# The product of the S5 state with C two chunks later in TensorE's program

## The chip, the cores and the metric

The kernel runs on one core of a Trainium2 chip. The time is the device time of one execution in microseconds (us); less is better. The engines are TensorE (PE; its weight loads are listed as PEld), VectorE (DVE), ScalarE (ACT), GpSimd (POOL) and SyncE (SP), which issues the loads. Each runs its own program in order and waits for the others by semaphores.

## The reference

Two blocks follow each other on a sequence of 256 tokens of width 2048. The first is a hybrid layer with three branches (a spatial gating, an S5 state space branch, a cross attention over 256 memory rows), gates and an output product; the second a convolution module and a squared-ReLU MLP. The change touches the S5 branch alone:

```python
lam_bar = jnp.exp(lam * dt)
b_bar = ((lam_bar - 1) / lam)[:, :, None] * b_mat
bu = jnp.einsum('bsgh,gph->bsgp', uf.astype(jnp.complex64), b_bar)
_, states = lax.associative_scan(combine, (a_el, bu), axis=1)
y = jnp.einsum('bsgp,ghp->bsgh', states, c_mat).real + d.astype(f32) * uf
y = jax.nn.gelu(y.reshape(bsz, seq, BRANCH_W)).astype(u.dtype)
return y * jax.nn.sigmoid(y @ glu_w + glu_b)
```

There are 64 groups of 16 channels with 64 complex states each.

## The kernel before

Activations stand transposed, channels on partitions and the 256 tokens along the free dimension. All weights stream through the core once, in 680 **chunks** of 128 x 1024 numbers (512 KB). `plan()` writes their order out; chunk `c` is the unit of every engine's program, and each engine has a loop over `c`:

- SyncE loads chunk `c` into one of seven `raw` slots (`s_raw`) once chunk `c - 7` has been used.
- ScalarE writes the high part `wh` (L522, `s_hi`), into one of four slots, so the high part of chunk `c + 3` waits until TensorE has finished chunk `c - 1` (`s_mm`).
- VectorE subtracts and writes the low part `wl` (L875, `s_low_v`); it does so for chunk `c + 3` at the beginning of its step `c`. (In two other stages GpSimd does this.)
- TensorE waits for the low part of chunk `c` and multiplies: for most chunks eight pairs, `wh` by both parts of the activation (L1580) and `wl` by the high part (L1582).

Then, still in step `c`, ScalarE and VectorE evacuate the output tile that ended with chunk `c - 1` (L531, L906), apply gates (L537 and L911, L915; L587 and L948, L956, L959), and do the small work of the stage, in an order written out by hand: the softmax of the cross attention at steps 112 to 159, GELU from step 168 on (every 11 steps one tile), and S5.

The S5 branch runs at steps 81 to 240 (`S5 = 81`, `S5_STEP = 5`), beside the weight products of other branches. Its 32 groups of states take five steps each: group `n` is at step `i` when `c - 81 = 5 n + i`. Four groups make a tile `tt`. Its parts:

- `bu(tt)` on TensorE ahead of chunk 81 + 20 tt: the products of the input with B for four groups, into banks 3 to 6 (L1603).
- `s5_main` on VectorE: at i = 1 two multiplications read the group's bank (L1178, L1179; the second tells `s_m`); at i = 2 two sums and two scans (L1182 to L1188); at i = 3 two multiplications (L1193, L1194; the second tells `s_n`, after which GpSimd's `tables` may go on); at i = 4 the two state tiles are written (L1203, L1204, `s_n4`), after a wait for the previous tile's product with C (`s_cy`), which reads the same states. The first group of a tile uses bank 6.
- `cy(tt)` on TensorE: the product of the four groups' states with C, eight matmuls (16 rows of the trace) into bank 6 (L1614). It waits for the tile's last states (`s_n4`) and, by `s_m >= 4 tt + 5`, for the next tile's first group to have been read out of bank 6. It stands ahead of chunk 81 + 20 (tt + 1) + 2, that is 103, 123, 143, 163, 183, 203 and 223, and the eighth, for which no group follows, ahead of chunk 243.
- `s5_out(tt)` on VectorE: one instruction (L1208) adds the skip term and takes the product out of bank 6, in step i = 3 of the next tile's first group (L1190, L1191), the eighth time in step 244. It tells `s_s5y`, for which `bu(tt + 2)` and ScalarE's GELU of this tile wait, the last GELU in its step 245.

Of the kernel before, what the change touches and what calls it, by code (L numbers as in the profile page):

```python
# [136 lines left out]
def end(stage, t):  # L137
    return AT[stage, t].end
# [18 lines left out]
S5_SET, S5_SIN, S5_STEP = 50, 67, 5  # L157
BIAS = 36
S5 = 81
# [81 lines left out]
def _build(nc, a, out, ctx):  # L241
# [101 lines left out]
    def cv(name, i=0):  # L343
        off = C_OFF[name][0] + i
        return cst[:, off:off + 1]
# [7 lines left out]
    def states(tt, q):  # L353

        return wn[q] if q < 2 else (wn_early if tt < 4 else wn_late)[q - 2]
# [512 lines left out]
    def vector(e):  # L868
        w = Waits(e)

        def low(c):
            if c in ON_POOL:
                return
            w.wait_ge(s_hi, c + 1)
            e.tensor_tensor(wl[:, c % RAW, :], raw[:, c % RAW, :], wh[:, c % WN, :].bitcast(F32),  # L875
                            ALU.subtract).then_inc(s_low_v, 1)

        def tree():
            n = 16
            while n > 2:  # L880
                n //= 2
                e.tensor_tensor(sq0[:, 0:n, :], sq0[:, 0:n, :], sq0[:, n:2 * n, :], ALU.add).then_inc(s_v, w.own())  # L882
                w.wait_ge(s_v, w.n)
            e.tensor_tensor(sq0[:, 0:1, :], sq0[:, 0:1, :], sq0[:, 1:2, :], ALU.add).then_inc(s_sum, 1)

        def rstd(n, dst, eps):
            w.wait_ge(s_mean, n)
            e.tensor_scalar(dst, bank[7][:, 0:T], eps, None, ALU.add).then_inc(s_eps, 1)
            w.wait_ge(s_root, n)
            e.reciprocal(dst, dst).then_inc(s_rstd, 1)  # L890
# [275 lines left out]
        def s5_main(c):  # L1166
            n, i = divmod(c - S5, S5_STEP)
            tt, q = n // 4, Q_ORDER[n % 4]
            k, bv = 4 * tt + q, bank[S5_BANK[q]].rearrange("p (r t) -> p r t", r=2)
            cb = wcs[n % 2][:, 0:1, :].broadcast_to((128, 2, T))  # L1170
            sb = wcs[n % 2][:, 1:2, :].broadcast_to((128, 2, T))
            if i == 1:
                w.wait_ge(s_bu, tt + 1)
                w.wait_ge(s_tab, n + 1)
                w.wait_ge(s_s5, 1)
                if n >= 1:
                    w.wait_ge(s_n4, n)
                e.tensor_tensor(wm1, bv, cb, ALU.mult).then_inc(s_v, w.own())  # L1178
                e.tensor_tensor(wm2, bv, sb, ALU.mult).then_inc(s_m, 1)  # L1179
            elif i == 2:  # L1180
                w.wait_ge(s_m, n + 1)
                e.tensor_tensor(wm1[:, 0, :], wm1[:, 0, :], wm2[:, 1, :], ALU.add).then_inc(s_v, w.own())  # L1182
                e.tensor_tensor(wm1[:, 1, :], wm1[:, 1, :], wm2[:, 0, :], ALU.subtract).then_inc(s_v, w.own())
                rb = rr[:, k:k + 1].broadcast_to((128, T))
                w.wait_ge(s_v, w.n - 1)
                e.tensor_tensor_scan(wsc[:, 0, :], rb, wm1[:, 0, :], 0.0, ALU.mult, ALU.add).then_inc(s_v, w.own())
                w.wait_ge(s_v, w.n - 1)
                e.tensor_tensor_scan(wsc[:, 1, :], rb, wm1[:, 1, :], 0.0, ALU.mult, ALU.add).then_inc(s_v, w.own())  # L1188
            elif i == 3:
                if n >= 4 and n % 4 == 0:  # L1190
                    s5_out(tt - 1)  # L1191
                w.wait_ge(s_v, w.n)
                e.tensor_tensor(wm1, wsc, cb, ALU.mult).then_inc(s_v, w.own())  # L1193
                e.tensor_tensor(wm2, wsc, sb, ALU.mult).then_inc(s_n, 1)  # L1194
            elif i == 4:
                w.wait_ge(s_n, n + 1)
                w.wait_ge(s_cy, tt)
                if tt >= 4:
                    w.wait_ge(s_sc, 8)
                else:  # L1200
                    w.wait_ge(s_mm, end("v", 1))
                st = states(tt, q)
                e.tensor_tensor(st[:, 0, :], wm1[:, 0, :], wm2[:, 1, :], ALU.subtract).then_inc(s_v, w.own())  # L1203
                e.tensor_tensor(st[:, 1, :], wm1[:, 1, :], wm2[:, 0, :], ALU.add).then_inc(s_n4, 1)  # L1204

        def s5_out(t):
            w.wait_ge(s_cy, t + 1)
            e.scalar_tensor_tensor(uT[:, t, :], uT[:, t, :], cv("d", t), bank[6][:, 0:T], ALU.mult,  # L1208
                                   ALU.add).then_inc(s_s5y, 1)
# [239 lines left out]
        for c in range(1, NC + 1):  # L1449
            if c + 3 < NC and c != POST:  # L1450
                low(c + 3)
            if c == RX:
                rstd(1, r_x, 1e-6)
            if c in ENDED:
                evac(ENDED[c])
            if RX < c <= RX + 10:
                w.wait_ge(s_rstd, 1)
                scaled(c - RX - 1, Xf, "pre", r_x, s_xn, s_hh, hp, s_hl)
            if c == MEM_SQ + 4:
                w.wait_ge(s_mq, 4)  # L1460
                tree()
            if c == MEM_R:
                rstd(2, r_mem, 1e-6)
            if MEM_N <= c < MEM_N + 10:
                w.wait_ge(s_rstd, 2)
                scaled(c - MEM_N, Mf, "memg", r_mem, s_mn, s_mh, mp, s_ml)
            if S5_SET <= c <= S5_SIN:
                next(main_setup, None)
                if c == S5_SIN:
                    for _ in main_setup:  # L1470
                        pass
            if S5_SIN < c < S5:
                next(main_scales, None)
            if BIAS <= c <= BIAS + 4:
                bias_row(c)
            if LN_V <= c < Z:
                norm_v(c)
            if Z <= c < Z + 8:
                spatial(c)
            if ATT <= c < ATT + 48:  # L1480
                softmax(c)
            if S5 <= c < S5 + 32 * S5_STEP:
                s5_main(c)
            if c == S5 + 32 * S5_STEP + 3:
                s5_out(7)
            if GELU <= c < GELU + 8 * GELU_STEP:
                gelu(c)
            if c - 1 in ENDED and ENDED[c - 1].stage == "b1":
                t = ENDED[c - 1].t
                w.wait_ge(s_mgh, t + 1)  # L1490
                w.wait_ge(s_mg, 32 + t + 1)
                e.scalar_tensor_tensor(mgp.lo[:, t, :], Mf[:, t, :], 0.5, mgp.hi[:, t, :].bitcast(F32), ALU.mult,
                                       ALU.subtract).then_inc(s_mgl, 1)
            if c - 2 in ENDED and ENDED[c - 2].stage == "out" and c <= POST:
                out_second(ENDED[c - 2].t)
            if c - 1 in ENDED and ENDED[c - 1].stage == "out" and c <= POST:
                out_first(ENDED[c - 1].t)
            if OUT + 8 <= c < OUT + 24:
                t = c - OUT - 8
                w.wait_ge(s_xsq, t + 1)  # L1500
                if t == 0:
                    e.tensor_scalar(extra[1], scrB[7], 1.0, None, ALU.mult).then_inc(s_xsum, 1)
                else:
                    w.wait_ge(s_xsum, t)
                    e.tensor_tensor(extra[1], extra[1], scrB[7], ALU.add).then_inc(s_xsum, 1)
            if c == POST:
                out_first(15)
                out_second(15)
                post(c)
                e.tensor_scalar(cvs("wdw"), cvs("wdw"), 0.5, None, ALU.mult).then_inc(s_wdw, 1)  # L1510
            if c == POST + 1:
                w.wait_ge(s_w62h, 1)
                e.tensor_tensor(w62[1], cst[:, C_OFF["wdw"][0] + 14 * 31:C_OFF["wdw"][0] + 16 * 31],
                                w62[0].bitcast(F32), ALU.subtract).then_inc(s_w62l, 1)
            if P1 <= c <= P1_END:
                taps(c)
            if c in (PIVOT + 1, PIVOT + 2):
                centre(4 * (c - PIVOT - 1), 4)
            if c == LN2:
                norm_conv()  # L1520
            if c == FFN + 3:
                rstd(5, keep[1], 1e-5)
# [7 lines left out]
    def tensor(e):  # L1530
# [154 lines left out]
        for c in range(NC):  # L1685
# [14 lines left out]
            if Z <= c < Z + 8 and (c - Z) % 2 == 0:  # L1700
                i = (c - Z) // 2
# [12 lines left out]
            if S5 <= c < S5 + 32 * S5_STEP:  # L1714
                n, i = divmod(c - S5, S5_STEP)
                if i == 0 and n % 4 == 0:
                    bu(n // 4)
                if i == 2 and n % 4 == 0 and n >= 4:
                    cy(n // 4 - 1)
            if c == S5 + 32 * S5_STEP + 2:  # L1720
                cy(7)
            if c == POST:
                w.wait_ge(s_psum, 16)
# [110 lines left out]
```

## Time and profile before

| what | value |
|---|---|
| three runs | 2154.38, 2166.30, 2165.95 us, median 2165.95 us |
| the profiled execution | 2151.97 us, span 2150.2 us |
| TensorE, VectorE, ScalarE, GpSimd busy | 2025.2, 1653.2, 1015.5, 406.3 us |
| mean granted TensorE clock | 0.973 of full speed |
| S5 stage, first `bu` to last `cy` | 262 to 822 us of the span |
| there: TensorE, VectorE busy | 510.62 and 482.69 of 560 us, granted clock 0.96 |

Full speed of the clock is 2.4 GHz; 0.5 would be 1.2 GHz throughout. Times in the trace are from the start of the span. In a row of the timeline the bracket at the end is the idle time of that engine just before the instruction and what ended it.

### The profile page before, as it was taken

What the parts mean: (1) busy time and instruction counts of PE and PEld (TensorE: products, weight loads), DVE (VectorE), ACT (ScalarE), POOL (GpSimd) and SP (SyncE); (2) the same over time, 40 slices, a digit from 0 to 9 for tenths busy, and PEclk for the clock granted to TensorE, in tenths of its full rate; (3) what the DMA queues carried; (4) which work ended last, traced back from release to release, by engine and by line L of the source; (5) the groups of instructions that cost most, each with busy time, mean ns of one, the idle gap of its engine ahead of it and who ended that gap; (6) DMA issues with size and microseconds to landing.
All of it is one profiled execution on the core that took longest, in us unless ns stands there. A gap on an engine that the chain in (4) does not pass through costs nothing.

```text
span 2150.2 us, 30509 instructions
## 1 busy us (share of the span) xinstructions
PE 2025.2 (94%) x11898; PEld 1766.3 (82%) x11898; DVE 1653.2 (77%) x2630; ACT 1015.5 (47%) x1561; POOL 406.3 (19%) x281
## 2 busy tenths in 40 slices
PE   7899998999878989999889997999999999999997
PEld 6788887778767878888679996888888888888886
DVE  8766798988789986687889997777657656756765
ACT  5544443444433445556556634545434434434542
POOL 3400233433233330000158860000000000000000
PEclk9999999999989999999989998999999999999998
DMA  7554554444434545566435540555556555565563
GB/s 294 191 180 160 189 180 147 148 147 157 146 119 147 177 151 182 186 206 206 157 119 186 182 143 15 191 187 192 190 188 191 189 189 193 188 192 189 188 193 119
DMA packets 101519, 370.46 MB, mean 172 GB/s; under 512 B 11392, under 2 KB 11392, under 8 KB 101376
## 3 DMA queue, kind: packets, MB, share of 16 engines
q1 hardware_dynamic: 101376, 368.52, 52.6%
q8 instruction: 94, 1.54, 0.3%
q14 instruction: 49, 0.40, 0.1%
HBM read 366.38 MB, written 2.10 MB: 171 GB/s over the span
## 4 chain that ended last, share of the span: by engine, by line
PE 64%; DVE 27%; ACT 4%; issue 3%; DMA 1%; SPq 0%; DVEq 0%; ACTq 0%
PE bank L1580 38%; PE bank L1582 19%; DVE wl L875 7%; DVE bank L1382 6%; ACT wh L522 2%; PE bank L1570 1%; PE bank L1569 1%; PE bank L1571 1%; DVE scr L906 1%; DVE upad L988 1%; DVE sq L882 1%; DVE wm L1178 1%; PE bank L1614 1%; DVE wm L1179 1%; PE bank L1664 1%
## 5 line engine op out<-in xcount | busy, mean ns | idle before, releaser
L875 DVE TENSOR_TENSOR wl<-raw,wh 128x1024 fp32r<-128x1024 f32 x598 | 750.7, 1259 | 362.3 <-ACT wh L522 361.2
L522 ACT ACTIVATE wh<-raw 128x1024 fp32r<-128x1024 f32 x680 | 712.1, 1055 | 538.1 <-PE bank L1582 434.5
L1580 PE MATMUL bank<-Hr,wh 128*128 128x512 f32 x2432 | 869.8, 402 | 10.3 <-DVE wl L875 6.2
L1580 PE MATMUL bank<-Yr,wh 128*128 128x512 f32 x2240 | 792.3, 398 | 25.2 <-DVE wl L875 11.0
L1582 PE MATMUL bank<-Hr,wl 128*128 128x256 f32 x2432 | 683.5, 281 | 0.0
L1582 PE MATMUL bank<-Yr,wl 128*128 128x256 f32 x2240 | 626.8, 280 | 0.0
L1580 PEld LDWEIGHTS bank<-Hr,wh 128*128 128x128 f32 x2432 | 462.6, 190 | 129.0 <-issue 8.7
L1580 PEld LDWEIGHTS bank<-Yr,wh 128*128 128x128 f32 x2240 | 423.1, 189 | 129.6 <-DVE wl L875 11.4
L1582 PEld LDWEIGHTS bank<-Hr,wl 128*128 128x128 f32 x2432 | 464.1, 191 | 0.3
L1582 PEld LDWEIGHTS bank<-Yr,wl 128*128 128x128 f32 x2240 | 424.7, 190 | 0.2
L474 POOL TENSOR_TENSOR wl<-raw,wh 128x1024 fp32r<-128x1024 f32 x82 | 204.6, 2503 | 391.4 <-ACT wh L522 391.3
L1382 DVE SCALAR_TENSOR_TENSOR bank<-upad,cst,bank 128x256 f32<-128x256 f32 x406 | 164.9, 480 | 0.8
L1585 PE MATMUL bank<-Hr,wh 128*128 128x256 f32 x512 | 147.5, 288 | 12.2 <-DVE Hr L1361 11.5
L1586 PE MATMUL bank<-Hr,wh 128*128 128x256 f32 x512 | 146.2, 286 | 0.0
L1587 PE MATMUL bank<-Hr,wl 128*128 128x256 f32 x512 | 146.2, 285 | 0.0
L489 POOL TENSOR_TENSOR wcs<-tab 128x256 f32<-128x256 f32 x32 | 40.6, 1268 | 486.4 <-DVE wm L1194 344.3
L1585 PEld LDWEIGHTS bank<-Hr,wh 128*128 128x128 f32 x512 | 99.5, 194 | 14.1 <-issue 7.8
L1586 PEld LDWEIGHTS bank<-Hr,wh 128*128 128x128 f32 x512 | 99.7, 195 | 0.0
L1587 PEld LDWEIGHTS bank<-Hr,wl 128*128 128x128 f32 x512 | 99.7, 195 | 0.0
L665 ACT ACTIVATE Yr<-scrB 128x256 fp32r<-128x256 f32 x64 | 26.8, 418 | 146.6 <-DVE scrB L1018 146.6
L587 ACT ACTIVATE scr<-scr 128x256 f32<-128x256 f32 x32 | 13.4, 418 | 97.8 <-DVE scr L906 97.8
L1021 DVE TENSOR_TENSOR Yr<-scrB,Yr 128x256 fp32r<-128x256 f32 x64 | 27.2, 425 | 31.0 <-ACT Yr L665 31.0
(287 smaller groups left out, 1756.5 us busy)
## 6 DMA issues: line engine op xcount, KB each, us to landing
raw<-in_w_up SPq DMA_DIRECT2D x128, 512.0 KB, 4.3
raw<-in_w_dn SPq DMA_DIRECT2D x128, 512.0 KB, 4.3
raw<-in_w_g SPq DMA_DIRECT2D x96, 512.0 KB, 3.7
raw<-in_w_p SPq DMA_DIRECT2D x96, 512.0 KB, 3.7
raw<-in_w_b SPq DMA_DIRECT2D x48, 512.0 KB, 3.7
raw<-in_w_out SPq DMA_DIRECT2D x32, 512.0 KB, 4.3
raw<-in_w_bx SPq DMA_DIRECT2D x16, 512.0 KB, 4.9
raw<-in_w_q SPq DMA_DIRECT2D x16, 512.0 KB, 3.9
```

Of the source, the lines that this page charges most:

```text
L474: e.tensor_tensor(wl[:, c % RAW, :], raw[:, c % RAW, :], wh[:, c % WN, :].bitcast(F32), ALU.subtract).then_inc(s_low_g, 1)
L489: e.tensor_tensor(d[:, 0, :, :], *sides(0, 0), ALU.mult)
L522: e.activation(wh[:, c % WN, :], raw[:, c % RAW, :], ACT.Copy).then_inc(s_hi, 1)
L665: e.activation(hid.hi[:, t % 16, :], kept(j), ACT.Copy).then_inc(s_hidh, 1)
L875: e.tensor_tensor(wl[:, c % RAW, :], raw[:, c % RAW, :], wh[:, c % WN, :].bitcast(F32), ALU.subtract).then_inc(s_low_v, 1)
L1021: e.tensor_tensor(hid.lo[:, t % 16, :], s, hid.hi[:, t % 16, :].bitcast(F32), ALU.subtract).then_inc(s_hidl, 1)
L1382: e.scalar_tensor_tensor(ac, pad[:, j:j + T], wj, ac, ALU.mult, ALU.add).then_inc(s_v, w.own())
L1580: e.matmul(dst.rearrange("p (h t) -> p h t", h=2), lh, pair.both[:, :, k, :], start=first_part and kk == 0, stop=last_part and kk == 7, sk ...
L1582: ins = e.matmul(dst[:, 0:T], ll, pair.hi[:, k, :], start=False, stop=last_part and kk == 7, skip_group_check=True)
L1585: e.matmul(dst[:, 0:T], lh, pair.hi[:, k, :], start=first_part and kk == 0, stop=False)
L1586: e.matmul(dst[:, 0:T], lh, pair.lo[:, k, :], start=False, stop=False)
L1587: ins = e.matmul(dst[:, 0:T], ll, pair.hi[:, k, :], start=False, stop=last_part and kk == 7)
```

## The change

`cy` moves from step i = 2 to step i = 4 of the next tile's first group in TensorE's program, so behind two more chunks (ahead of chunks 105, 125, 145, 165, 185, 205 and 225); the eighth moves from chunk 243 to 244. `s5_out` moves from i = 3 of that group to i = 1 of the one after it, three steps later, the eighth time from step 244 to 245. The waits inside the functions stay.

```diff
@@ s5_main (VectorE)
             if i == 1:
+                if n >= 5 and n % 4 == 1:
+                    s5_out(tt - 1)
                 w.wait_ge(s_bu, tt + 1)
@@
             elif i == 3:
-                if n >= 4 and n % 4 == 0:
-                    s5_out(tt - 1)
                 w.wait_ge(s_v, w.n)
@@ vector
-            if c == S5 + 32 * S5_STEP + 3:
+            if c == S5 + 32 * S5_STEP + 4:
                 s5_out(7)
@@ tensor
                 if i == 0 and n % 4 == 0:
                     bu(n // 4)
-                if i == 2 and n % 4 == 0 and n >= 4:
+                if i == 4 and n % 4 == 0 and n >= 4:
                     cy(n // 4 - 1)
-            if c == S5 + 32 * S5_STEP + 2:
+            if c == S5 + 32 * S5_STEP + 3:
                 cy(7)
```

## Rows read from the trace of the kernel before

**Rows 1.** The page's sums: busy us (share of the span), instructions.

```profile
PE 2025.2 (94%) x11898; PEld 1766.3 (82%) x11898; DVE 1653.2 (77%) x2630; ACT 1015.5 (47%) x1561; POOL 406.3 (19%) x281
```

**Rows 2.** TensorE's waits, 260 to 870: total us, times, longest us.

```profile
PE bank L1614 <- DVE wm L1179: 33.9, 6, 7.3
PE bank L1580 <- DVE wl L875: 5.3, 6, 1.6
```

**Rows 3.** Windows, the six idle stretches: length, busy us of each engine, clock, DMA.

```profile
core 0: us, PE busy (x) PEld busy (x) DVE busy (x) ACT busy (x) POOL busy (x), PEclk, DMA share, GB/s
328.64:335.77 7.13, 0.00 (x1) 0.03 (x1) 6.96 (x10) 3.21 (x5) 2.37 (x4) 0.78 0.22 75
469.18:471.67 2.49, 0.01 (x1) 0.04 (x2) 2.27 (x6) 1.36 (x3) 0.00 (x0) 1.00 0.59 194
...
755.67:761.60 5.93, 0.00 (x0) 0.03 (x1) 5.86 (x8) 2.35 (x4) 3.42 (x4) 0.81 0.27 92
sum 33.90, PE 0.01 PEld 0.19 DVE 29.39 ACT 14.93 POOL 10.45; mean PE 0.00 PEld 0.03 DVE 4.90 ACT 2.49 POOL 1.74
```

**Rows 4.** Windows, product and next chunk at these six sites.

```profile
471.67:477.10 5.43, 5.43 (x33) 4.25 (x34) 3.50 (x7) 0.15 (x1) 0.00 (x0) 0.69 0.04 16
...
761.60:767.58 5.98, 5.98 (x33) 4.20 (x33) 3.17 (x6) 0.72 (x2) 0.00 (x0) 0.62 0.00 0
sum 36.05, PE 36.04 PEld 25.89 DVE 20.49 ACT 2.02 POOL 0.00; mean PE 6.01 PEld 4.32 DVE 3.42 ACT 0.34 POOL 0.00
```

**Rows 5.** Windows, product and next chunk at the eighth site.

```profile
821.38:825.32 3.94, 3.94 (x34) 2.98 (x34) 2.51 (x3) 1.37 (x2) 0.00 (x0) 1.00 0.44 140
```

**Rows 6.** Timeline of VectorE, 328 to 343: start, us, instruction.

```profile
331.29 2.35 DVE L875 TENSOR_TENSOR wl<-raw,wh 128x1024 fp32r<-128x1024 f32 x2
...
334.94 0.68 DVE L1179 TENSOR_TENSOR wm<-bank,wcs 128x512 f32<-128x512 f32 x1
335.54 1.22 DVE L875 TENSOR_TENSOR wl<-raw,wh 128x1024 fp32r<-128x1024 f32 x1
```

**Rows 7.** Timeline of VectorE, its idle time behind the six stalls.

```profile
342.72 1.23 DVE L875 TENSOR_TENSOR wl<-raw,wh 128x1024 fp32r<-128x1024 f32 x1 [4.11 <-ACT wh L522]
...
478.45 1.22 DVE L875 TENSOR_TENSOR wl<-raw,wh 128x1024 fp32r<-128x1024 f32 x1 [3.06 <-ACT wh L522]
...
553.55 1.22 DVE L875 TENSOR_TENSOR wl<-raw,wh 128x1024 fp32r<-128x1024 f32 x1 [4.77 <-ACT wh L522]
...
631.55 1.22 DVE L875 TENSOR_TENSOR wl<-raw,wh 128x1024 fp32r<-128x1024 f32 x1 [4.51 <-ACT wh L522]
...
700.47 1.23 DVE L875 TENSOR_TENSOR wl<-raw,wh 128x1024 fp32r<-128x1024 f32 x1 [2.74 <-ACT wh L522]
...
768.93 1.23 DVE L875 TENSOR_TENSOR wl<-raw,wh 128x1024 fp32r<-128x1024 f32 x1 [4.16 <-ACT wh L522]
```

**Rows 8.** Timeline of ScalarE, 341 to 342.

```profile
341.63 1.06 ACT L522 ACTIVATE wh<-raw 128x1024 fp32r<-128x1024 f32 x1 [9.78 <-PE bank L1582]
```

**Rows 9.** Timeline of TensorE, its waits for VectorE between the stalls.

```profile
378.76 0.44 PE L1635 MATMUL bank<-ident,Pb 128*128 128x128 f32 x2 [2.45 <-DVE Pb L1288]
...
578.24 0.51 PE L1580 MATMUL bank<-Hr,wh 128*128 128x512 f32 x1 [0.45 <-DVE wl L875]
...
669.45 0.50 PE L1580 MATMUL bank<-Hr,wh 128*128 128x512 f32 x1 [0.26 <-DVE wl L875]
...
742.83 0.50 PE L1580 MATMUL bank<-Hr,wh 128*128 128x512 f32 x1 [1.15 <-DVE wl L875]
```

**Rows 10.** Timelines of VectorE and TensorE: chunk 242's low part and first matmul.

```profile
814.81 1.22 DVE L875 TENSOR_TENSOR wl<-raw,wh 128x1024 fp32r<-128x1024 f32 x1
...
818.46 0.40 PE L1580 MATMUL bank<-Hr,wh 128*128 128x512 f32 x1
```

**Rows 11.** Line L1208: duration min/median/max ns, first and last start.

```profile
L1208 DVE SCALAR_TENSOR_TENSOR uT<-uT,cst,bank x8: 472/475/477, 346.1 to 828.1; 128x256 f32<-128x256 f32 x8
```

**Rows 12.** Windows, 570 to 610.

```profile
570.00:610.00 40.00, 33.15 (x177) 27.43 (x177) 34.92 (x56) 18.49 (x33) 11.45 (x12) 0.96 0.45 145
```

## The prediction

> **What bounds the kernel now.** I read the page's sums first. TensorE is busy for 94% of the span and VectorE for 77% [rows 1]: the kernel is TensorE's, but a share over 2150 us says nothing about one stage, so the next view is who TensorE waits for in the S5 stage. There one line stands out: 33.9 us in front of the product with C (L1614), in six of its eight calls, and each time the releaser is L1179, VectorE's second multiplication out of bank 6 [rows 2]. In the code this is the wait of `cy` for `s_m`: the product writes bank 6 and may not start before step i = 1 of the next group has read it. `cy` stands ahead of chunk 5n+2 of the stage where n is a multiple of 4, and that reading belongs to VectorE's step just one chunk earlier, so VectorE has less than one chunk for it. The waits for the low parts of the weights (L875) come to only 5.3 us [rows 2].
>
> The stretches themselves say more. Six idle stretches sum to 33.90 us, and VectorE is busy for 29.39 us of them [rows 3]: it is not idling, it is behind. The clock pays too. From the start of the product to the end of the chunk behind it the six stalled sites take 36.05 us, at granted clocks like 0.62 and 0.69 [rows 4]; the last site, which did not wait, takes 3.94 us at 1.00 [rows 5]. So 36.05 - 6 x 3.94 = 12.4 us goes to matmuls at 1.2 instead of 2.4 GHz after the idling. At most 33.9 + 12.4 = 46.3 us is to be had.
>
> What can be had depends on VectorE. After a stall it runs out of work: it waits 4.11, 3.06, 4.77, 4.51, 2.74 and 4.16 us for the first high part that ScalarE could not write while TensorE stood still, in sum 23.4 us [rows 7]; ScalarE had waited 9.78 us for TensorE at the first of them [rows 8]. Between the stalls VectorE loses that lead again, until TensorE waits for it: for a softmax weight behind the first site (2.45 us), for low parts behind the third, fourth and fifth (0.45, 0.26, 1.15 us) [rows 9]. Where such a tie comes before the next site, the gain is what VectorE gained, not what TensorE gained.
>
> **The change, part by part.** *The product moves two chunks later.* There are eight: the six that stall, and two that don't. It asks for the same `s_m` with two chunks more to cover it. One chunk at full clock takes 3.94 us less about 1.0 us for the product, so 2.9 us [rows 5]. The first site worked out: TensorE ends chunk 102 at 328.64, takes chunk 103 at once until 331.5, waits about 1 us for chunk 104's low part (the first of the pair that ends at 333.64), ends chunk 104 at 335.4 and finds L1179 done at 335.62 [rows 3, 6]. So 7.13 us of idle time go, about 1.2 us of new waits come, and with the site's share of the clock, 12.4 / 6 = 2.1 us, TensorE wins about 8 us. VectorE, though, wins 4.11 us [rows 7], and the tie at 378.76 [rows 9] hands on only that.
>
> The six sites, in order:
> - site at 335.77: 4.1 us (VectorE's idle time, tie at 378.76);
> - site at 471.67: 2.49 us idle [rows 3] + 5.43 - 3.94 = 1.5 us of clock [rows 4, 5] = 4.0 us. VectorE is not behind here (it idles 3.06 us after the stall, and more later), so TensorE keeps all of it;
> - site at 545.94: 4.8 us (tie at 578.24);
> - site at 623.55: 4.5 us (tie at 669.45);
> - site at 692.99: 2.7 us (tie at 742.83);
> - site at 761.60: 5.93 us idle + 5.98 - 3.94 = 2.0 us of clock, less about 0.3 us of new wait, is 7.6 us; VectorE gains 4.16 us and had a lead of 818.46 - 816.03 = 2.4 us at the thinnest place, chunk 242, whose low part is the fifteenth after the one at 768.93 [rows 7, 10]. So 4.2 + 2.4 = 6.6 us.
>
> Sum: 4.1 + 4.0 + 4.8 + 4.5 + 2.7 + 6.6 = 26.7, say **27 us**. Lower bound: VectorE's idle time alone, 23.4 us. Upper bound: 46.3 us less the new waits at the new place, about 1 us at four sites, so 42 us. I take 27, near the lower end, since three ties in a row show VectorE as the limit between 570 and 745.
>
> *What asks for the product.* VectorE's step i = 4 waits for `s_cy` before it overwrites the states that the product reads. Before, this product was two chunks old; now TensorE issues it in the very step. Queued behind that wait are the next low part and so TensorE. The cover: this step begins with a low part whose high part needs the chunk ahead of the product, and these two take 1.06 + 1.22 us [rows 7, 8] against about 1.0 us for the product. No cost; without the cover at most 1 us x 8. The step works later than that wherever VectorE is behind.
>
> *The evacuation (L1208, 475 ns [rows 11]) moves from step 3 to step 1 of the next group.* The same eight instructions, 3.8 us, on the same engine. They leave the way of L1193/L1194, which release GpSimd's tables, and enter that of L1178/L1179 of a group whose readers are no longer close. Between -0.5 and +0.5 us at each of eight sites; I take 0. The next product with B (`bu`) waits for `s_s5y` 14 chunks later. The eighth evacuation now falls in the VectorE step in which ScalarE's last GELU asks for it, one step earlier before: ScalarE may wait one low part and the evacuation, 1.22 + 0.48 = 1.7 us, with the next high part queued behind. TensorE gets no stall from this while low parts are 2 us ahead: 0, at most 1.7 us. No DMA is moved; the weight loads hang on `s_mm`, and follow the chunks.
>
> **Against the times.** The profiled execution takes 2151.97 us, 1.8 us over its span; with the sum it would take 2125 us. The shown median, 2165.95 us, lies 14 us above it. I carry the difference over: 2166 - 27 = **2139 us**, a gain of 1.25%.
>
> **Rivals.**
> *All of it is kept (TensorE is the limit).* If VectorE finds slack where TensorE runs into it, 42 us: 2124 us. For it: 5.3 us only of waits for low parts over the stage. Against it: these waits are few because the six stalls refill VectorE's lead. 12%.
> *The wait comes back.* VectorE is busy for 34.92 of 40 us between 570 and 610 [rows 12], and part of its remaining idle time comes from round trips through ScalarE which no earlier TensorE shortens. If half of the 23.4 us goes the same way, 12 us stay: 2154 us, within 1%. Against it: the idle times of rows 7 end on a high part that waited for TensorE alone. 18%.
> *Slower, by the clock.* The six long waits become many short ones in front of low parts. If TensorE then ran at 1.2 GHz through the tied stretches, it would fall behind VectorE. A product with its chunk at a granted 0.62 takes 5.98 against 3.94 us [rows 4, 5], 2.0 us more; 13 such chunks undo the 27 us, and 24 of the 120 between the first and the last stalled product make it 1% slower, 2188 us. Against it: from 570 to 610 TensorE already waits in this way, busy for 33.15 of 40 us, and the granted clock is 0.96 [rows 12]. 5%.
> The Trainium skill ("TensorE: Matmul & The Clock Gate", section "A second HAM failure mode: psum-queue depth-cycling") tells of a kernel whose TensorE idled briefly between groups of matmuls so often that the clock swung between its two levels and throughput fell. By that rule the tied stretches would swing too, and the sum would end near the 2188 us of this rival; the trace shows it only in small, with 0.96.
> *It does nothing.* Were the true releaser another semaphore, asked for as late at the new place, the time stays: 2166 us, 3%. Against it: `s_n4`, the other wait of `cy`, is told by a step two before that of L1179, and the profile names L1179 six times in six [rows 2].
>
> **How the numbers follow.** Forecast 62%. A measurement of this kernel tells about 1% (22 us) from no change. Of the forecast's own range, 20 to 34 us, a little lies below that; with the full gain this makes faster 0.68, within 1% 0.27, slower 0.05. The range runs from 2112 us (the full gain of 42 us on a run like the lowest one shown, 2154) to 2154 us (half of it given back); beyond it lie the slower case, no effect, and the poorer half of the third.
>
> **What the changed profile should show.** The 33.9 us in front of L1614 fall under 5 us, and the granted clock behind the products is mostly 1.00. VectorE's six idle times of rows 7 are gone or under 2 us. TensorE's other waits for VectorE grow by 10 to 19 us (46.3 us that were lost less 27 us won), above all for L875, in the stretches behind the stalled products. The S5 stage, from the first `bu` to the last `cy`, gets shorter by 27 us, and nothing else changes. Wrong would be: a wait of VectorE at L1203 for the product; a granted clock under 0.9 over whole stretches; or L875 waits of 30 us, which would mean that VectorE's own work, not the place of one wait, sets the stage.

## The result, and the profile after

The changed kernel takes 2124.41 us (median of 4, 2123.11 to 2138.78) beside 2160.16 us for the kernel before (median of 4); the ratio is 0.9875, with a 95% interval from 0.9838 to 0.9912. (The quotient of the two medians alone would be 0.983; 7 to 27 later executions of the kernel before have medians of 2151.47 to 2151.99 us, and beside those the change wins 27 us.) Its profiled execution takes 2123.11 us, its span 2121.4 us against 2150.2 us: 28.8 us less, where the sum had said 27. Single runs of either kernel now and then take some 13 us more (2154 and 2166 us before, 2123 and 2139 us after), and in the one that was traced (2140.26 us, with the product one chunk later) the loss of 13.4 us lies between chunks 400 and 679, behind the S5 stage, so experiments are compared below by stretches of their traces as well as by medians.

The page's sums of the changed kernel, which answer to [rows 1]:

```profile
PE 2018.8 (95%) x11898; PEld 1759.5 (83%) x11898; DVE 1653.4 (78%) x2630; ACT 1013.6 (48%) x1561; POOL 405.4 (19%) x281
```

VectorE does the same work in less time. Who TensorE waits for in the S5 stage (260 to 870; total us, times, longest), to be read beside [rows 2]:

```profile
PE bank L1580 <- DVE wl L875: 11.9, 13, 1.8
PE bank L1580 <- DVE Yr L915: 4.0, 2, 2.8
PE bank L1635 <- DVE Pb L1288: 3.6, 2, 3.2
PE bank L1580 <- DVE scr L906: 2.9, 7, 0.9
...
PE bank L1614 <- DVE wm L1181: 1.1, 1, 1.1
```

The 33.9 us in front of the product are 1.1 us now (L1181 is the old L1179). What has grown stands above it: many short waits for VectorE, none longer than 3.2 us. The windows from the product to the end of the chunk behind it, at the six sites of [rows 4] (first, last, sum):

```profile
334.84:338.76 3.92, 3.92 (x32) 3.02 (x33) 3.92 (x7) 0.00 (x0) 0.00 (x0) 1.00 0.43 138
...
739.80:743.73 3.93, 3.93 (x33) 2.97 (x33) 3.88 (x8) 2.89 (x5) 0.00 (x0) 1.00 0.42 141
sum 23.51, PE 23.51 PEld 17.92 DVE 22.68 ACT 9.50 POOL 0.86; mean PE 3.92 PEld 2.99 DVE 3.78 ACT 1.58 POOL 0.14
```

They take 23.51 us instead of 36.05, at a granted 1.00: the clock's share, 12.5 us, is back. VectorE's idle times of [rows 7] are gone too; from the first site on, its longest wait for a high part is 1.74 us:

```profile
604.51 1.23 DVE L875 TENSOR_TENSOR wl<-raw,wh 128x1024 fp32r<-128x1024 f32 x1 [1.74 <-ACT wh L522]
```

Where the time was won is read from the first matmul (L1580) of the same chunk in both traces:

| chunk | before | after | won so far | won since the row above | forecast |
|---|---|---|---|---|---|
| 101 (ahead of the first site) | 322.72 | 321.77 | 0.95 | | |
| 117 (behind the tie on the softmax) | 382.55 | 377.38 | 5.17 | 4.2 | 4.1 |
| 161 | 535.61 | 525.28 | 10.33 | 5.2 | 4.0 |
| 181 | 610.96 | 595.67 | 15.29 | 5.0 | 4.8 |
| 201 | 679.91 | 659.95 | 19.96 | 4.7 | 4.5 |
| 221 | 749.75 | 728.30 | 21.45 | 1.5 | 2.7 |
| 246 (behind the stage) | 830.96 | 801.50 | 29.46 | 8.0 | 6.6 |

The first 0.95 us lie ahead of any edit, and the rest of the program gives back 0.6 us: neither is the change's. The stage wins 28.5 us.

### The profile page after: what moved, and what is told of

Its sections match the earlier page's. It is cut to its first block, busy times and chain, and to the rows that moved or that the text cites. A ratio compares the mean times of both kernels' runs of the same rounds, so it can differ in the third digit from the quotient of the medians.

```text
span 2121.4 us, 30516 instructions
## 1 busy us (share of the span) xinstructions
PE 2018.8 (95%) x11898; PEld 1759.5 (83%) x11898; DVE 1653.4 (78%) x2630; ACT 1013.6 (48%) x1561; POOL 405.4 (19%) x281
## 4 chain that ended last, share of the span: by engine, by line
PE 67%; DVE 26%; ACT 3%; issue 3%; DMA 0%; SPq 0%; DVEq 0%; ACTq 0%
PE bank L1580 40%; PE bank L1582 20%; DVE bank L1382 6%; DVE wl L875 6%; ACT wh L522 2%; PE bank L1571 1%; PE bank L1569 1%; PE bank L1570 1%; DVE scr L906 1%; DVE upad L988 1%; DVE sq L882 1%; PE bank L1664 1%; DVE wm L1180 1%; DVE wsc L1190 1%; DVE wsc L1188 1%
## 5 line engine op out<-in xcount | busy, mean ns | idle before, releaser
L1580 PE MATMUL bank<-Hr,wh 128*128 128x512 f32 x2432 | 863.9, 400 | 17.4 <-DVE wl L875 11.9
L1580 PE MATMUL bank<-Yr,wh 128*128 128x512 f32 x2240 | 793.2, 399 | 28.4 <-DVE wl L875 10.9
L1580 PEld LDWEIGHTS bank<-Hr,wh 128*128 128x128 f32 x2432 | 458.7, 189 | 137.7 <-issue 12.2
L1580 PEld LDWEIGHTS bank<-Yr,wh 128*128 128x128 f32 x2240 | 423.2, 189 | 133.3 <-DVE wl L875 11.3
L587 ACT ACTIVATE scr<-scr 128x256 f32<-128x256 f32 x32 | 13.4, 418 | 115.3 <-DVE scr L906 115.3
```

The lines of the kernel that those rows point to most:

```text
L1580: e.matmul(dst.rearrange("p (h t) -> p h t", h=2), lh, pair.both[:, :, k, :], start=first_part and kk == 0, stop=last_part and kk == 7, sk ...
```

## The experiments

**The product alone.** The product two chunks later, the evacuation left at step 3 of the group, where it now asks for a product that TensorE issues one step later. Against the changed kernel:

```diff
             if i == 1:
-                if n >= 5 and n % 4 == 1:
-                    s5_out(tt - 1)
...
             elif i == 3:
+                if n >= 4 and n % 4 == 0:
+                    s5_out(tt - 1)
...
```

> The product with C two chunks later as in the change, its evacuation left in step i = 3, so that VectorE now asks for the product in the step just before TensorE issues it. My theory (the gain comes from the product no longer waiting for bank 6): the whole gain of 26 to 29 us stays, the time in front of L1614 is under 3 us; VectorE waits 1 to 2 us in front of L1208 at the two or three sites where it is not behind, covered by low parts that are 5 us ahead. Rival (the order on VectorE does it, because the evacuation leaves the way of the table release): most of the gain is gone, span above 2140.

Measured: 2124.34 us, ratio 0.987 (0.9839 to 0.9901), by the medians the same as the whole change. By its trace the stage wins 26.2 us instead of 28.5; in it the granted clock fell twice where it did not with the whole change, behind the softmax waits that end at 372.53 and 513.47 (0.69 and 0.57 over the next 4 us). TensorE's and VectorE's waits in the stage:

```profile
PE bank L1614 <- DVE wm L1179: 1.0, 1, 1.0
```

```profile
DVE uT L1208 <- PE bank L1614: 1.7, 1, 1.7
```

The evacuation has to wait once, 1.7 us, at 405.77, where VectorE is not behind; TensorE does not notice. So the second half of the change is not needed for the gain. (One such wait came, where two or three were expected.)

**The evacuation alone.** The product ahead of chunk 5n + 2 as before, the evacuation three steps later. Against the changed kernel:

```diff
-                if i == 4 and n % 4 == 0 and n >= 4:
+                if i == 2 and n % 4 == 0 and n >= 4:
                     cy(n // 4 - 1)
...
```

> Only the evacuation three steps later, the product where it was. My theory: nothing, span 2148 to 2152, 33 to 35 us in front of L1614 as before. Rival (order on VectorE): 10 us or more faster.

Measured: 2152.63 us, ratio 1.0002 (0.9981 to 1.0023). TensorE's waits show the old stall whole:

```profile
PE bank L1614 <- DVE wm L1181: 33.6, 6, 7.1
```

**One chunk instead of two.** Against the changed kernel:

```diff
-                if i == 4 and n % 4 == 0 and n >= 4:
+                if i == 3 and n % 4 == 0 and n >= 4:
                     cy(n // 4 - 1)
```

> The product one chunk later instead of two, the evacuation as in the change. My theory: every wait in front of L1614 shrinks by about one chunk, 2.9 us (7.1 to 4.2, 2.5 to 0, 4.4 to 1.5, 6.7 to 3.8, 7.3 to 4.4, 5.9 to 3.0: 17 us in sum), and since that is less than or like VectorE's idle time behind each stall nearly all of it is handed on: gain 16 to 22 us, span 2128 to 2134. Rival (the clock after long idling is what the stalls really cost): four waits above 3 us stay, so the clock falls as often and the gain is under 10 us. Second rival (VectorE is the only limit): half of 23.4 us, about 12.

Measured: 2127.95 us, ratio 0.9895 (0.9852 to 0.9938). Behind the stage its trace has won 25.1 us, of which 1.2 us lie ahead of the first site: 24 us. The timeline of TensorE, the starts of the five products that still wait (the idle time in brackets):

```profile
334.64 0.59 PE L1614 MATMUL bank<-wn,Cs 128*32 128x256 f32 x2 [4.33 <-DVE wm L1181]
...
537.57 0.41 PE L1614 MATMUL bank<-wn,Cs 128*32 128x256 f32 x2 [1.58 <-DVE wm L1181]
...
610.27 0.64 PE L1614 MATMUL bank<-wn,Cs 128*32 128x256 f32 x2 [5.46 <-DVE wm L1181]
...
675.19 0.41 PE L1614 MATMUL bank<-wn,Cs 128*32 128x256 f32 x2 [3.88 <-DVE wm L1181]
...
740.82 0.58 PE L1614 MATMUL bank<-wn,Cs 128*32 128x256 f32 x2 [3.10 <-DVE wm L1181]
```

18.4 us of waits stay where 17 were expected, within 0.6 us of the forecast at each site but 610.27 (5.46 instead of 3.8). The gain is 2 us above the expected range. Both rivals fall: waits of 3 to 5 us remain and most of the gain is there, so the clock is not what the stalls mainly cost; and 24 us is twice what the second rival gave. The first chunk brings 24 us, the second 4.5.

**Four chunks.** Two more than in the change, with the evacuation at step 3 of the group after. Against the changed kernel:

```diff
-                if i == 4 and n % 4 == 0 and n >= 4:
+                if i == 1 and n % 4 == 1 and n >= 5:
                     cy(n // 4 - 1)
```

> The product four chunks later than before (two more than in the change), the evacuation at step 3 of the next group. My theory: TensorE has nothing more to win in front of L1614 (about 1 us is left), while VectorE's step 4 (L1203) now asks for a product that is issued two chunks later: waits of 2 to 5 us in front of L1203 where VectorE is not behind, next to none where it is. Low parts are 4 to 7 us ahead at those sites, so most of it is covered: 0 to 10 us slower than the change, span 2121 to 2132. Rival (later is simply better or free): span within 2 us of the change or below.

Measured: 2128.76 us, ratio 0.989 (0.9852 to 0.9927); by the trace the stage wins 23.8 us instead of 28.5. VectorE's waits show the consumer's side:

```profile
DVE wnE L1203 <- PE bank L1614: 8.0, 2, 4.2
```

The wait of step 4 for the product, which cost nothing at two chunks, costs 8.0 us of VectorE at two sites, and the stage wins 4.7 us less. Of the places tried (none, one, two and four chunks later) two chunks is the best; three was not tried.

**Another bank instead of another place.** Product and evacuation where they were before; for tiles 0 and 3 to 7 the product goes to bank 7, free at those times, and asks no `s_m`. Against the kernel before:

```diff
-            w.wait_ge(s_m, min(4 * tt + 5, 32))
+            if tt in (1, 2):
+                w.wait_ge(s_m, min(4 * tt + 5, 32))
+            else:
+                w.wait_ge(s_z, 4)
+                w.wait_ge(s_s5y, tt)
+                if tt >= 3:
+                    w.wait_ge(s_o, 8)
...
-                    ins = e.matmul(bank[6][32 * q:32 * q + 32, 0:T], Cs[:, r, 4 * tt + q, :], states(tt, q)[:, r, :],
+                    ins = e.matmul(bank[6 if tt in (1, 2) else 7][32 * q:32 * q + 32, 0:T], Cs[:, r, 4 * tt + q, :], states(tt, q)[:, r, :],
```

(The evacuation reads the same bank, and the first softmax waits for `s_s5y` once.)

> The kernel before, product and evacuation where they were, but for the tiles 0 and 3 to 7 the product goes to bank 7, which is free then, so that it needn't wait for bank 6 to be read (s_m); it still waits for its states (s_n4). Tiles 1 and 2 stay as before. My theory (the cause is the wait for bank 6, not the place): in front of L1614 about 8 us are left: 2.7 at the first site and 2.8 at 692.99, where L1204 ends that much after TensorE is free (331.36 and 688.51 against 328.64 and 685.73), 2.5 at the untouched site at 471.67, none at the other three; gain 20 to 26 us, span 2124 to 2130. Rival (the place in TensorE's program matters for another reason): above 2140.

Measured: 2129.63 us, ratio 0.989 (0.9874 to 0.9907), 21.8 us less than before by the medians. TensorE's waits (L1620 is the product):

```profile
PE bank L1620 <- DVE wnL L1204: 2.9, 2, 2.7
PE bank L1620 <- DVE wnE L1204: 2.8, 1, 2.8
PE bank L1620 <- DVE wm L1179: 2.3, 1, 2.3
```

That is the forecast 8 us, split as forecast: the states at two sites, bank 6 at the untouched one. Most of the gain is there without the product's moving in TensorE's program: the place matters through the wait for bank 6.

**Low parts on GpSimd.** The step "VectorE is the limit behind the sites" was tried by freeing VectorE, on the changed kernel and on the one before.

```diff
-ON_POOL = {c for c in range(4, 32, 2)} | set(range(P1, P1_END + 4))
+ON_POOL = {c for c in range(4, 32, 2)} | set(range(89, 241, 5)) | set(range(P1, P1_END + 4))
```

> The change, and one in five low parts of the S5 stage (chunks 89, 94, ... 239) on GpSimd instead of VectorE. My theory (after the change VectorE is the limit in the tied stretches, and the gain stops where VectorE's lead is used up): VectorE is freed of 31 x 1.25 us, loses part of it to slower instructions beside GpSimd, and TensorE's remaining waits for it, 24 us in the stage, shrink by a third to a half: 8 to 15 us faster than the change, span 2106 to 2114. Rival (TensorE itself or ScalarE's chain is the limit): within 3 us of the change.

> The kernel before with the same move of low parts to GpSimd. My theory: the waits in front of L1614 come from VectorE being behind, so they shrink from 33.9 us toward what is left when it is not behind (2.5 to 4.5 us a site, 15 to 22 us in sum): span 2128 to 2140, so 10 to 22 us faster than before, and the change is still worth 20 us or more on top of it. Rival (the stall is only a matter of the place in the program): the sum in front of L1614 stays above 30 us.

Measured: 2137.16 us on the changed kernel (ratio to before 0.9919, 0.9891 to 0.9946), so 13 us slower than the change; 2161.96 us on the kernel before (1.0049, 1.0022 to 1.0076), 10 us slower than it. Both expectations missed, and on the changed kernel the rival too: VectorE was not freed. Its groups in the stage, first in the changed kernel, then in the same with low parts on GpSimd (busy us, mean ns):

```profile
L948 DVE SCALAR_TENSOR_TENSOR Mf<-scr,Mf 128x256 f32<-128x256 f32 x16 | 6.9, 431 | 0.5
L956 DVE SCALAR_TENSOR_TENSOR scr<-scr,scr 128x256 f32<-128x256 f32 x16 | 7.0, 435 | 0.6
```

```profile
L956 DVE SCALAR_TENSOR_TENSOR scr<-scr,scr 128x256 f32<-128x256 f32 x16 | 17.4, 1089 | 0.5
L948 DVE SCALAR_TENSOR_TENSOR Mf<-scr,Mf 128x256 f32<-128x256 f32 x16 | 13.6, 849 | 0.6
```

These two alone give back 17 of the 39 us, and the windows over the S5 stage show that all of it is given back. VectorE is busy for 480.41 us in the changed kernel and for 482.92 us with 31 low parts fewer (the third pair of numbers):

```profile
262.00:792.00 530.00, 502.00 (x2909) 420.64 (x2902) 480.41 (x731) 231.74 (x385) 185.74 (x180) 0.99 0.50 161
```

```profile
262.00:806.00 544.00, 505.63 (x2913) 424.28 (x2906) 482.92 (x700) 232.03 (x385) 248.82 (x212) 0.98 0.47 157
```

The timeline of the same kernel shows how:

```profile
621.72 2.41 POOL L474 TENSOR_TENSOR wl<-raw,wh 128x1024 fp32r<-128x1024 f32 x1 [12.24 <-ACT wh L522]
...
622.04 2.37 DVE L956 SCALAR_TENSOR_TENSOR scr<-scr,scr 128x256 f32<-128x256 f32 x1
```

An instruction of 0.42 us that starts during GpSimd's ends 0.3 us behind it. On the kernel before, the sign that the rival had named came, over 30 us in front of the product:

```profile
PE bank L1614 <- DVE wm L1179: 30.9, 6, 7.5
```

But since VectorE was not freed, this decides nothing against the first reading, and the pair does not settle the question of the limit; the next three bear on it. (Why the sum comes out slower, not merely even, I did not trace to the end. TensorE's direct waits for GpSimd are 4.0 us of it.)

**More work for VectorE.** The four multiplications of a group are done twice, in groups 20 to 27 and in groups 8 to 15 of the changed kernel, and in groups 20 to 27 of the kernel before.

```diff
             if i == 1:
...
+                if 20 <= n < 28:
+                    e.tensor_tensor(wm1, bv, cb, ALU.mult).then_inc(s_v, w.own())
+                    e.tensor_tensor(wm2, bv, sb, ALU.mult).then_inc(s_v, w.own())
+                    w.wait_ge(s_v, w.n)
                 e.tensor_tensor(wm1, bv, cb, ALU.mult).then_inc(s_v, w.own())
                 e.tensor_tensor(wm2, bv, sb, ALU.mult).then_inc(s_m, 1)
...
             elif i == 3:
+                if 20 <= n < 28:
+                    e.tensor_tensor(wm1, wsc, cb, ALU.mult).then_inc(s_v, w.own())
+                    e.tensor_tensor(wm2, wsc, sb, ALU.mult).then_inc(s_v, w.own())
+                    w.wait_ge(s_v, w.n)
```

> The change, with VectorE's four multiplications of a group (L1180, L1181 and the two after the scans) done twice in groups 20 to 27, where TensorE waits for VectorE. They take 0.60 to 0.68 us each, 2.4 to 2.7 us a group, 19 to 22 us in all. My theory (VectorE sets the pace there): nearly all of it is paid, 16 to 22 us slower than the change, span 2138 to 2144. Rival (TensorE sets the pace and VectorE's time is hidden): under 5 us.

> The same doubling in groups 8 to 15, where low parts are 5 to 9 us ahead and VectorE idles about 12 us in front of L875. My theory: two thirds or more hidden, 2 to 8 us slower than the change, span 2123 to 2130. Rival (VectorE sets the pace of the whole stage): 16 us or more as in the other stretch.

> The kernel before with VectorE's four multiplications done twice in groups 20 to 27, as it was done to the changed kernel, where it cost 19.9 us. My theory: VectorE's idle time behind a stall is the stall's own echo and no reserve, since a later L1179 makes the stall longer by as much: 17 to 21 us slower than before. Rival (VectorE's idle time behind the stalls at 623.55 and 692.99, 7.3 us, absorbs part): 13 us or less.

Groups 20 to 27 of the changed kernel: 2144.48 us (ratio 0.9945, 0.9924 to 0.9967), 20 us slower than the change; its trace has lost 19.8 us behind the stage. All of it is paid, and TensorE's waits (L1588 is its first matmul of a pair) grow where they should:

```profile
PE bank L1588 <- DVE wl L875: 17.2, 15, 2.3
PE bank L1588 <- DVE scr L906: 9.9, 14, 0.9
PE bank L1622 <- DVE wm L1185: 5.1, 3, 2.3
```

Even the wait in front of the product (L1622) is back at three sites, 5.1 us instead of 1.1.

Groups 8 to 15: 2137.96 us (0.9938, 0.9917 to 0.9958), 13.6 us slower than the change, 13.9 us by the trace from chunk 117 to 246. I had expected 2 to 8, and the rival said 16 or more: two thirds are paid. Low parts are far ahead there, but another path ties TensorE to VectorE. Its waits from 395 to 545 in the changed kernel, and from 400 to 560 with the extra work:

```profile
PE bank L1644 <- ACT pT L685: 1.8, 1, 1.8
PE bank L1628 <- ACT qT L690: 0.3, 1, 0.3
```

```profile
PE bank L1643 <- DVE Pb L1296: 5.7, 3, 2.3
PE bank L1652 <- ACT pT L685: 3.6, 3, 2.1
PE bank L1636 <- ACT qT L690: 3.3, 2, 2.6
```

Every one of these is the softmax (scores to VectorE, to ScalarE, to VectorE, back to TensorE), which goes round in fixed chunks and has no lead. They are 10.5 us longer than in the changed kernel. Behind two of them the granted clock fell (0.57 over the 4 us from 447.72, 0.60 over those from 528.97), which I estimate from these two numbers at 3.3 us more; together that is about the 13.9 us.

Groups 20 to 27 of the kernel before: 2170.96 us (1.0089, 1.0074 to 1.0104), 19.5 us slower than before. The 7.3 us that VectorE idles behind the two stalls there absorb little; 6.2 us of them are still there:

```profile
629.96 1.22 DVE L875 TENSOR_TENSOR wl<-raw,wh 128x1024 fp32r<-128x1024 f32 x1 [3.80 <-ACT wh L522]
```

```profile
708.58 1.22 DVE L875 TENSOR_TENSOR wl<-raw,wh 128x1024 fp32r<-128x1024 f32 x1 [2.43 <-ACT wh L522]
```

TensorE's waits, in front of the product (L1622) and of the chunks (L1588):

```profile
PE bank L1622 <- DVE wm L1183: 40.2, 6, 9.9
PE bank L1588 <- DVE wl L875: 9.9, 8, 2.3
PE bank L1588 <- DVE scr L906: 4.3, 6, 1.0
```

The time came out as expected, the way to it only in part. A VectorE that is later makes the stalls longer, but by 6.3 us in sum and not by the whole; the waits for low parts and evacuations between the stalls (5.3 and 0.4 us before) grow by 8.5 us. What holds is that the idle time comes from the stall (in the changed kernel it is gone with it), and that work added elsewhere on VectorE hardly falls into it.

## Why the prediction was right, point by point

**The wait.** Right: the bank 6 wait costs 33.9 us, and all but about 1 us of it goes when the place changes (the product alone, which is 27.7 us faster than before). All but the forecast 8 us goes when the bank changes (21.8 us faster), and nothing when the evacuation moves.

**The clock.** Right in size: 36.05 to 23.51 us is 12.5 us, forecast 12.4. Over chunks 101 to 246 as a whole, though, TensorE is busy for 453.01 us instead of 460.14, 7.1 us less; in which other chunks the rest of the 12.5 us was spent again was not traced.

**What is handed on.** Right: 28.5 us of the 46.3 us. The ties are where they were forecast, and the segments from 101 to 117, 161 to 181 and 181 to 201 come within 0.2 us of VectorE's idle time behind the stall [rows 7]. That VectorE, not TensorE, then sets the pace is shown for groups 20 to 27 by the doubled multiplications (19.8 us paid of 19 to 22).

**Segments off.** Up to chunk 161 5.2 us instead of 4.0. 1.5 us of that lie in chunk 158: before, it ran behind a softmax wait of 2.15 us at a granted 0.64 and took 4.69 us; after, behind one of 1.78 us at 1.00, it takes 3.2 us. From 201 to 221 1.5 us instead of 2.7, because the reverse happens at chunk 219: behind a wait of 1.77 us it takes 4.6 us at 0.63, where it took 3.1 us before. The two rows, chunk 158 before and chunk 219 after:

```profile
523.40:528.09 4.69, 4.69 (x19) 4.03 (x18) 4.66 (x9) 0.50 (x2) 0.00 (x0) 0.64 0.01 4
```

```profile
719.84:724.47 4.63, 4.63 (x17) 3.95 (x18) 4.40 (x7) 3.06 (x6) 0.00 (x0) 0.63 0.18 73
```

Neither is a term of the sum. The last segment wins 8.0 us instead of 6.6; that it gets back there what chunk 219 lost is my reading, and no run tests it. That the sum of 26.7 us lies within 2 us of 28.5 is in part luck: the second segment is 1.2 us over its forecast and the fifth 1.2 us under.

**The waits that remain.** Forecast 10 to 19 us more. The rows above show 11.9 + 4.0 + 3.6 + 2.9 = 22.4 us, where the kernel before had 11.4 us of the same: 11 us more, at the low end.

**The covers.** The asking wait of step 4 costs nothing at two chunks, as argued, and 8.0 us of VectorE at four. The evacuation's move costs nothing that the medians show and brings nothing by itself. The wait that was priced at 1.7 us at most, ScalarE's for the eighth evacuation, came at that size, and TensorE got no stall from it:

```profile
ACT Pb L718 <- DVE uT L1208: 1.7, 1, 1.7
```

**The clock rival.** The granted clock over the tied stretches is 1.00, 0.95, 1.00 and 0.98 (windows of the changed kernel, from 330 to 376, 560 to 592, 610 to 672 and 680 to 722):

```profile
330.00:376.00 46.00, 39.78 (x231) 32.84 (x230) 42.72 (x66) 20.25 (x32) 15.58 (x14) 1.00 0.47 152
560.00:592.00 32.00, 25.06 (x128) 20.54 (x128) 27.57 (x44) 13.28 (x24) 11.44 (x12) 0.95 0.37 123
610.00:672.00 62.00, 57.81 (x327) 48.00 (x326) 59.10 (x88) 24.74 (x42) 23.03 (x24) 1.00 0.51 162
680.00:722.00 42.00, 38.10 (x202) 31.03 (x201) 39.71 (x61) 16.87 (x30) 18.09 (x18) 0.98 0.51 165
```

So TensorE did not run at 1.2 GHz through the tied stretches. The clock does fall behind single short waits: behind 1.77 us for a low part (the row of chunk 219 above) and behind 2.84 us for a gate at 586.94 (0.57 over the next 4 us), but not behind 1.65 us for a low part at 567.74. The length of the wait does not decide it alone. The same wait of 3.17 us for a softmax weight was followed by 1.00 in the changed kernel and by 0.69 in the product alone:

```profile
373.59:377.60 4.01, 4.01 (x23) 3.53 (x24) 3.98 (x7) 3.01 (x5) 2.78 (x3) 1.00 0.00 1
```

```profile
372.53:376.53 4.00, 4.00 (x17) 3.48 (x18) 3.97 (x7) 2.38 (x4) 2.77 (x3) 0.69 0.00 1
```

The Trainium skill's swing between the levels ("TensorE: Matmul & The Clock Gate", section "A second HAM failure mode: psum-queue depth-cycling") came in this small measure only, with 0.95 at the lowest over a tied stretch.

**The base.** The one step that was off: the 14 us between the profiled execution and the median were carried over to the forecast. The profile's own sum, 2125 us, is what came (2124.41). The shown median of three lay 14 us above the profiled execution of the kernel before; the medians of 7 to 27 later executions of it, 2151.47 to 2151.99 us, lie on it. So the forecast of 2139 us was 15 us too high, and the time that came, 2124 us, is the one named for the rival that keeps all of it. That is a coincidence of the base: that rival needed a gain of 42 us, and the stage won 28.5.

**A claim that fell.** That TensorE keeps everything at the site at 471.67 "because VectorE is not behind" was right in its number and too simple in its reason: VectorE's work is not hidden there either, as the extra work in groups 8 to 15 shows. There the softmax passes it on.

## What to carry to other kernels

A wait in one engine's program is judged by who sets its releaser, and how many steps lie between: here one step was too few, two chunks more were enough, and four ran into the consumer's own wait. How much of a removed stall reaches the end is read from the other engine: the idle time that follows the stall on it, up to the next place where the first engine waits for it, forecast three of the six segments to within 0.2 us. Idle time that follows a stall is not a reserve: about 20 us of extra work on VectorE in the kernel before cost 19.5 us, and the idle time behind the stalls stayed.

## What the runs showed of the hardware

Here a VectorE instruction on two SBUF tiles that starts during a subtraction on GpSimd does not end before it: L956 takes 0.42 us alone and 2.37 us when it starts 0.3 us into a subtraction of 2.41 us. In all ten such cases of L948 and L956 in that trace it ends 0.28 to 0.29 us behind GpSimd's. I had counted on losing a part of the 39 us that were moved, and the kernel came out 13 us slower. The Trainium skill ("SBUF — State Buffer", section "Who interferes with whom") says that a VectorE instruction with two SBUF inputs contends with a GpSimd instruction that reads SBUF, that the ports which the two engines share are an exclusive lock, and that the order of issue decides who blocks; the trace agrees, with these numbers.
